# Stick-breaking suffix sums as high and low parts in single-pass matmuls, and the eviction of u moved to VectorE

## The reference

```python
z = jnp.einsum('bqhd,bkhd->bhqk', qb, kb).astype(jnp.float32) * scale
mask = k_pos < q_pos
log_beta = jax.nn.log_sigmoid(z)
log_1m_beta = jnp.where(mask, jax.nn.log_sigmoid(-z), 0.0)
log_remain = lax.cumsum(log_1m_beta, axis=3, reverse=True) - log_1m_beta
att = jnp.where(mask, jnp.exp(log_beta + log_remain), 0.0)
outs.append(jnp.einsum('bhqk,bkhd->bqhd', att.astype(vb.dtype), vb))
...
u = u + (token_shift(u) - u) * mu
```

## Time and profile before

| | |
|---|---|
| median of 3 runs | 1917.1 us (1916.41 to 1917.37) |
| the profiled execution | 1921.47 us, its span 1919.6 us |
| TensorE matmuls, busy | 1825.8 us, 95% of the span |
| TensorE weight loads, busy | 1424.1 us, 74% |
| VectorE, busy | 936.3 us, 49% |
| ScalarE, busy | 697.5 us, 36% |
| GpSimd, busy | 135.3 us, 7% |
| mean TensorE clock granted | 0.98 |

### The profile page before, as it was taken

One profiled execution on the slowest core, in us unless ns is written; L12 is line 12 of the kernel. 1 busy time (PEld: TensorE's weight loads), 2 busy tenths in 40 slices (PEclk: granted clock), 3 DMA queues, 4 the chain that ended last, 5 costly groups with the idle time before them and its releaser, 6 DMA issues.

```text
span 1919.6 us, 27690 instructions
## 1 busy us (share of the span) xinstructions
PE 1825.8 (95%) x11652; PEld 1424.1 (74%) x11652; DVE 936.3 (49%) x1482; ACT 697.5 (36%) x1055; POOL 135.3 (7%) x109
## 2 busy tenths in 40 slices
PE   5998989979999998999999999899889899999999
PEld 2666655758888886788888887565778688888887
DVE  4267877364444344544244444445745544433442
ACT  4224547343323233433133334577311433312321
POOL 0013435200000002000000010000000010000000
PEclk8999999989999999999999999999999899999999
DMA  9663101112222222123223312101000222322231
GB/s 381 235 234 116 45 28 34 66 54 93 95 99 99 99 98 89 66 99 121 73 94 106 113 66 77 66 33 44 24 4 4 66 94 94 123 85 88 98 127 39
DMA packets 44475, 176.16 MB, mean 92 GB/s; under 512 B 5568, under 2 KB 5824, under 8 KB 41024
## 3 DMA queue, kind: packets, MB, share of 16 engines
q1 hardware_dynamic: 44352, 174.39, 26.3%
HBM read 168.34 MB, written 2.10 MB: 89 GB/s over the span
## 4 chain that ended last, share of the span: by engine, by line
PE 85%; DVE 7%; DMA 3%; ACT 3%; issue 2%; SPq 0%; DVEq 0%; ACTq 0%
PE bank L364 23%; PE bank L365 23%; PE bank L366 23%; DMA arena<-ada_late 1%; PE bank L508 1%; PE bank L524 1%; PE bank L540 1%; PE bank L715 1%; PE bank L856 1%; DMA arena<-ada 1%; PE bank L873 1%; PE bank L864 1%; DMA ring<-m_w_v 1%; ACT wsp L1087 1%; DVE arena L2052 1%
## 5 line engine op out<-in xcount | busy, mean ns | idle before, releaser
L1562 DVE TENSOR_TENSOR wsp<-ring,wsp 128x1024 fp32r<-128x1024 f32 (+2 forms) x244 | 312.7, 1283 | 442.4 <-ACT wsp L1087 442.3
L364 PE MATMUL bank<-hs,wsp 128*128 128x512 f32 x1160 | 472.8, 408 | 16.0 <-DVE hs L1829 5.3
L1087 ACT ACTIVATE wsp<-ring 128x1024 fp32r<-128x1024 f32 (+2 forms) x244 | 268.8, 1104 | 579.4 <-PE bank L366 573.4
L365 PE MATMUL bank<-hs,wsp 128*128 128x512 f32 x1160 | 455.0, 392 | 0.0
L366 PE MATMUL bank<-hs,wsp 128*128 128x512 f32 x1160 | 455.0, 392 | 0.0
L364 PEld LDWEIGHTS bank<-hs,wsp 128*128 128x128 f32 x1160 | 219.8, 190 | 87.2 <-issue 31.6
L365 PEld LDWEIGHTS bank<-hs,wsp 128*128 128x128 f32 x1160 | 220.1, 190 | 48.7 <-issue 5.7
L366 PEld LDWEIGHTS bank<-hs,wsp 128*128 128x128 f32 x1160 | 219.6, 189 | 47.1
L365 PE MATMUL bank<-hids,wsp 128*128 128x512 f32 x608 | 236.7, 389 | 0.0
L366 PE MATMUL bank<-hids,wsp 128*128 128x512 f32 x608 | 236.7, 389 | 0.0
L364 PE MATMUL bank<-hids,wsp 128*128 128x512 f32 x608 | 236.7, 389 | 0.0
(11 more groups left out here) (340 smaller groups left out, 2119.2 us busy)
## 6 DMA issues: line engine op xcount, KB each, us to landing
ring<-m_gate SPq DMA_DIRECT2D x44, 512.0 KB, 3.4
ring<-m_up SPq DMA_DIRECT2D x44, 512.0 KB, 3.4
ring<-m_down SPq DMA_DIRECT2D x32, 704.0 KB, 4.0
ring<-m_w_in SPq DMA_DIRECT2D x38, 512.0 KB, 3.5
arena<-ada_late SPq DMA_DIRECT2D x16, 1024.0 KB, 7.1
ring<-m_w_up SPq DMA_DIRECT2D x32, 512.0 KB, 3.4
ring<-m_w_down SPq DMA_DIRECT2D x32, 512.0 KB, 3.4
ring<-m_w_out SPq DMA_DIRECT2D x16, 512.0 KB, 3.7
```

The source lines that it names most:

```text
L364: pe.matmul(out, lhs[0], rhs[0], start=start, stop=False)
L365: pe.matmul(out, lhs[0], rhs[1], start=False, stop=False)
L1087: act.activation(wsp[:, s % SPLIT, 0, 0:size], ring[:, i % RING, 0:size], ACT.Copy)\
L1562: dve.tensor_tensor(wsp[:, s % SPLIT, 1, 0:size], ring[:, i % RING, 0:size], wsp[:, s % SPLIT, 0, 0:size].bitcast(F32), ALU.subtract).then ...
```

## The change

The softplus is kept as two fp32r tensors. VectorE writes it to raw_sp, ScalarE copies it to sp_hi (`sb_high`, new), VectorE subtracts sp_hi from raw_sp into sp_lo, which lies on the same memory as raw_sp. The sums take ramps, an fp32r copy of the two constant matrices, against the high parts of both heads, then against the low parts. The running sums (`presum`) are gone; instead each kind has a matmul per later group of key blocks, widened over unused columns to 256 where there is room. att is one buffer in tmp instead of three. The ScalarE queue gets `sb_high(n)` behind `sb_exp(n-1)`; logs wait for the suffix sum that last read sp_lo. u's first eviction goes from ScalarE to VectorE, as `tensor_scalar` ahead of the shift.

```diff
+        raw_sp = [area(at * K, (2, w)) for at, w in zip((34, 37, 40), WIDTH)]
+        sp_hi = [at(f"sp_hi{n}", [P, 2, w], F32R, arena_at + 4 * k * K)[0] for n, (k, w) in enumerate(zip((24, 27, 30), WIDTH))]
+        sp_lo = [at(f"sp_lo{n}", [P, 2, w], F32R, arena_at + 4 * k * K)[0] for n, (k, w) in enumerate(zip((34, 37, 40), WIDTH))]
+        ramps, _ = at("ramps", [P, 2, P], F32R, cst_at + 4 * CONST["suffix"][0])
+        att = tmp[:, 4:6, :]
...
             def sb_suffix(p):
-                pe.wait_ge(S("softplus"), p + 1)
-                if kind:
-                    pe.wait_ge(S("presum"), 2 * i + kind)
-                for e in range(2):
-                    b = set_of(p) + e
-                    pe.matmul(bank[:, b, 0:w], const("suffix"), sp[kind][:, e, :], start=False, stop=False,
-                              skip_group_check=True)
-                    later = (sp[0][:, e, 0:P], sp[0][:, e, P:3 * P], sp[1][:, e, :])[kind]
-                    at = w - (1, 2, 3)[kind] * P
-                    mm = pe.matmul(bank[:, b, at:w], const("minus"), later, start=False, stop=True,
-                                   skip_group_check=True)
+                later = (((0, 0, 2, 2),), ((0, 1, 1, 2), (0, 0, 2, 2)), ((1, 0, 1, 3), (0, 1, 2, 2), (0, 0, 3, 1)))[kind]
+                for part, v in enumerate((sp_hi, sp_lo)):
+                    if part == 0:
+                        pe.wait_ge(S("sp_hi"), p + 1)
+                    else:
+                        pe.wait_ge(S("softplus"), 2 * p + 2)
+                    for e in range(2):
+                        b = set_of(p) + e
+                        pe.matmul(bank[:, b, 0:w], ramps[:, 0, :], v[kind][:, e, :], start=False, stop=False,
+                                  skip_group_check=True)
+                        for of, at, to, n in later:
+                            mm = pe.matmul(bank[:, b, to * P:(to + n) * P], ramps[:, 1, :],
+                                           v[of][:, e, at * P:(at + n) * P], start=False,
+                                           stop=(part == 1 and of == 0 and at == 0), skip_group_check=True)
                 mm.then_inc(S("sb_suffix"), 1)
...
             def sb_logs(p):
                 if p >= 3:
-                    act.wait_ge(S("sb_pv"), p - 2)
+                    act.wait_ge(S("sb_suffix"), (p, p - 1, p - 2)[kind])
...
+            def sb_high(p):
+                act.wait_ge(S("softplus"), 2 * p + 1)
+                act.activation(sp_hi[p % 3][:, :, :], raw_sp[p % 3], ACT.Copy).then_inc(S("sp_hi"), 1)
...
             def sb_exp(p):
                 act.wait_ge(S("sb_suffix"), p + 1)
-                act.activation(att[kind], bank[:, b:b + 2, 0:WIDTH[kind]], ACT.Exp).then_inc(S("att"), 1)
+                if p:
+                    act.wait_ge(S("sb_pv"), p)
+                act.activation(att[:, :, 0:WIDTH[kind]], bank[:, b:b + 2, 0:WIDTH[kind]], ACT.Exp).then_inc(S("att"), 1)
...
                     sb_exp(n - 1)
+                if n < PARTS:
+                    sb_high(n)
...
-                act.wait_ge(S("u_full"), n + 1)
-                act.activation(u[:, RW_ORDER[n], :], bank[:, n % 2, :], ACT.Identity,
-                               scale=unmixed[:, RW_ORDER[n]:RW_ORDER[n] + 1]).then_inc(S("u_raw"), 1)
...
             def softplus(p):
-                if p >= 3:
-                    dve.wait_ge(S("sb_suffix"), p - 1)
+                own("softplus")
+                dve.wait_ge(S("sp_hi"), p + 1)
+                dve.tensor_tensor(sp_lo[kind][:, :, :], v, sp_hi[kind][:, :, :].bitcast(F32), ALU.subtract)\
+                   .then_inc(S("softplus"), 1)
...
             def token_mix(n):
-                dve.wait_ge(S("u_raw"), n + 1)
+                dve.wait_ge(S("u_full"), n + 1)
+                do(dve.tensor_scalar(f, bank[:, b, :], unmixed[:, RW_ORDER[n]:RW_ORDER[n] + 1], None, ALU.mult))
...
+            do(dve.tensor_copy(ramps[:, :, :].rearrange("p a b -> p (a b)"), cst[:, CONST["suffix"][0]:CONST["minus"][1]]))
             sb_step(0)
```

More of the change, by code:

```diff
@@ L169, in build @@
         arena, arena_at = at("arena", [P, 74 * 256])
-        cst, _ = at("cst", [P, NCONST])
+        cst, cst_at = at("cst", [P, NCONST])
         col, _ = at("col", [P, NCOLS])
@@ L269, in build @@
         WIDTH = (3 * P, 3 * P, T)
-        sp = [area(at * K, (2, w)) for at, w in zip((24, 27, 30), WIDTH)]
-        att = [area(at * K, (2, w)) for at, w in zip((34, 37, 40), WIDTH)]
+        raw_sp = [area(at * K, (2, w)) for at, w in zip((34, 37, 40), WIDTH)]
[3 more added lines that the diff above has]
+        att = tmp[:, 4:6, :]
         u = area(44 * K, (14, T))
@@ L734, in sb_pv @@
                         mm = pe.matmul(bank[DH * e:DH * e + DH, 6, c * P:T], vtok2[:, c, hh * DH:(hh + 1) * DH],
-                                       att[kind][:, e, at:at + w], start=(c == 3), stop=(c == 0), skip_group_check=True)
+                                       att[:, e, at:at + w], start=(c == 3), stop=(c == 0), skip_group_check=True)
                 mm.then_inc(S("sb_pv"), 1)
@@ L1341, in sb_logs @@
                 b, kind = 2 + 2 * (p % 2), p % 3
-                z, raw = att[kind], bank[:, b:b + 2, 0:WIDTH[kind]]
+                z, raw = raw_sp[kind], bank[:, b:b + 2, 0:WIDTH[kind]]
                 act.wait_ge(S("sb_masked"), p + 1)
                 if p >= 3:
-                    act.wait_ge(S("sb_pv"), p - 2)
+                    act.wait_ge(S("sb_suffix"), (p, p - 1, p - 2)[kind])
                 do(act.activation(z, raw, ACT.Abs))
@@ L1444, in _ @@
                     key_line(n - 8)
-                if n >= 10:
-                    act.wait_ge(S("knorm"), n - 9)
-                act.wait_ge(S("u_full"), n + 1)
-                act.activation(u[:, RW_ORDER[n], :], bank[:, n % 2, :], ACT.Identity,
-                               scale=unmixed[:, RW_ORDER[n]:RW_ORDER[n] + 1]).then_inc(S("u_raw"), 1)
                 if 1 <= n < 5:
@@ L1933, in sb_mask @@
                 own("sb_masked")
[L1935 to L1943, removed]
             def softplus(p):
@@ L1947, in softplus @@
                 dve.wait_ge(S("log1p"), p + 1)
-                if p >= 3:
-                    dve.wait_ge(S("sb_suffix"), p - 1)
-                dve.scalar_tensor_tensor(out=sp[kind], in0=bank[:, b:b + 2, 0:WIDTH[kind]], scalar=0.0, in1=att[kind],
+                v = raw_sp[kind]
+                dve.scalar_tensor_tensor(out=v, in0=bank[:, b:b + 2, 0:WIDTH[kind]], scalar=0.0, in1=v,
                                          op0=ALU.max, op1=ALU.add).then_inc(S("softplus"), 1)
+                own("softplus")
+                dve.wait_ge(S("sp_hi"), p + 1)
+                dve.tensor_tensor(sp_lo[kind][:, :, :], v, sp_hi[kind][:, :, :].bitcast(F32), ALU.subtract)\
+                   .then_inc(S("softplus"), 1)
                 own("softplus")
@@ L1962, in sb_step @@
                     sb_mask(n)
-                if 1 <= n <= PARTS and n % 3:
-                    presum(n - 1)
                 if n < PARTS:
```

## The result

The changed kernel takes 1936.15 us in the median of 5 runs (1926.88 to 1937.64), against 1917.1 before. The ratio is 1.0081, with a 95% interval of 1.0061 to 1.0100: slower, as forecast. The forecast was 1931, inside a range of 1921 to 1938. The profiled execution is the fastest of the five, 1926.88 us with a span of 1925.1. This makes the stage, read from a profile, the steadier measure of what happens in it, though not of the kernel's time. From the first part's activations to the start of the last shift of u it took 1368.66 - 1216.79 = 151.9 us before.

The account below looks back on a forecast made before the run. TensorE was taken to bound the stage's first half, VectorE the second, with the ScalarE-VectorE relay becoming the first half's bound. Relay 10.0, second half 2.2 and clock 1.6 gave +13.8 us: median 1931, range 1921 to 1938.

Parts of the forecast that it names:

- What bounds it: Suffix-sum stage: TensorE's time counts in its first half, VectorE's in the second; hardly any slack around 1250 us.
- TensorE's gaps between 1222 and the last sum: Sign of the forecast: TensorE idle 8 us or more in this stretch of the stage.
- The releaser: Sign of the forecast: ScalarE's exponential is what ends TensorE's idle waits before the last sum.
- the waits of 2 and 4 us: First half: TensorE would stop some 2 us for part 1's exponentials and 4 us for part 4's.
- TensorE's part: Suffix sums over four head pairs: TensorE gives back 3.6 us (6.0 with 128 columns at 0.07), if nothing makes it wait.
- The relay, +10.0: First half: alternating ScalarE and VectorE work on each part becomes the bound; last sum begins at 1320.8, before 1310.79.
- The share of the eviction: u's eviction on VectorE: 0.72 us per tile end in the relay; second half +2.2 us, tiles 8 to 11 adding 2.9.
- Clock, +1.6 once: TensorE's clock falls to the 1.2 GHz level after its new wait for part 4, losing 1.6 us once.
- The rival with falls at more stops (1937): Clock falls at parts 1, 4, 6 and 9: two more dips, 3.2 us, high prices 2.5; 1937 us, chance 0.13.
- TensorE's wait for shift 9: Sign of the forecast: TensorE waits 4 us for VectorE's shift 9 of u.
- The rivals of no change and of a gain: TensorE stays the bound: 1917 us, chance 0.12; faster, with cheap 128-column sums and hidden evictions: 1911.5 us, chance 0.05.
- The sum: Whole kernel: 10.0 + 2.2 + 1.6 = +13.8 us, all other work only shifting.

Follow-up runs that it names:

- kernel before with tile ends deferred: Kernel before, with VectorE's work at the end of tiles 0 to 5 moved behind the next part's mask: 1919.6 us, ratio 0.9993.

## Why the prediction came out as it did

- *What bounds it.* Right: TensorE in the first half before, the relay after, VectorE in the second half. One reading of rows is misnumbered: the exponentials that end at 1259.12 and the value matmuls at 1259.26 belong to part 4, not part 3; the slack of 0.1 us that I read from them stands. TensorE's gaps between 1222 and the last sum are 98.5 - 85.3 = 13.2 us by the busy column (at least 8 were expected). The releaser is not the one named: the exponentials released values by 0.3 us, and the waits of 2 and 4 us for those of parts 1 and 4 did not come, because TensorE was already held up at banks 6 and 7.
- *TensorE's part.* The saving was sized too low: 3.6 us were forecast, and the busy times above give 5.9, close to the 6.0 that I kept beside it. The sum of kind 1 took 1.71 us (1.7 forecast), and of kind 2 one pass took 1.33, both 2.7 (2.4 to 3.0 forecast). A group of 384, 256 and 128 columns took 1321.21 - 1320.86 = 0.35 us, which leaves 0.06 for 128 columns: I took 0.22 and should have taken 0.07. By the Trainium skill's four passes for full FP32 ("FP8 and Floating Point Precision", TensorE Precision Notes) it was a quarter of 0.22; the trace agrees. The time forecast would still not have been better by it: it would have lain 2 us lower, farther from what was measured.
- *The relay, +10.0.* The mechanism held, but **this term was mis-sized: the first half grew by 15.0**, where relay and clock together were to give 11.6. Its prices are right (high 0.84, low 0.96, eviction 0.74), and the first two groups miss by 0.3 and 0.7 us. The third misses by 3.1 and the fourth by 1.2. What failed is that I let only logs of kind 0 lead over TensorE. The orders on record have the new high part ahead of `osb_squares` and `osb_root`; I priced these as ScalarE's time alone, though they also free banks 6 and 7 for TensorE's values and kk product. The reordering of ScalarE alone recovers 3.1 us. From part 6 to 7 it took 12.55 us for 10.65, of which 1.74 are the mask's wait for scores.
- *The share of the eviction.* In the second half +2.2 was forecast, with 0.57 for the eviction of tile 7, whose row reads 0.67; measured are +2.7 after and 3.1 to 3.2 when the eviction is moved alone. In the first half the relay's sum held 0.72 us for each tile end, but taking it out returned 1.3 us in all.
- *Clock, +1.6 once.* This was too small. In the first half the clock stood at 0.50 from the first sum at 1216.15 up to 1222, and again behind both stops of 3.2 us; TensorE needed some 6.8 us more for the same work than at 0.98. How much of that is on the path no run tells, since none takes the clock apart from the stops. The rival with falls at more stops (1937) is nearest to the median, 1936.15. TensorE's wait for shift 9 was forecast at 4 us and is 4.13:

```profile
1356.95 0.80 PE L367 MATMUL bank<-hs,wsp 128*128 128x512 f32 x1 [4.13 <-DVE arena L1974]
```

- *The rivals of no change and of a gain.* Their mechanisms exist. They need the relay out of the way, which the change does not do; the version with high part, eviction and raw softplus moved does, and has a stage 1.5 us shorter than before.
- *The sum.* Its +13.8 is close to the 14.0 us by which the changed kernel's median lies above that of the kernel before when both run by turns. That is luck in part: the stage grew by 17.7, which the time does not show in full, and the forecast had put no change outside the stage.

In stage time the loss is 17.7 us: 9.6 for high and low part with their hand-overs, 3.5 for the eviction moved alone, and 4.6 for what is left between 155.4 and 160.0. The split depends on the order in which the pieces are taken: the eviction returns 4.5 us from the changed kernel and 5.8 once the high part is on VectorE. The memory shared by raw and low part accounts for 3.1 of the 4.6 if its worth in the changed kernel holds here; the other 1.5 I can't place (one att tile for all kinds is a candidate that was not tried). The median moved by 14.0 to 19.0 us against the kernel before on the respective chip.

## What to carry to other kernels

Cheaper work on the busiest engine pays only if what prepares it on the others stays shorter than that engine's time: lay out one round of the hand-overs, operation by operation, before trusting busy shares of 43% and 73%. In that round follow every bank and every buffer, not only the data: an operation put ahead of the one that frees a bank ties another engine in, and prices then no longer add. When the split is wanted, do softplus, high and low on one engine, which gave 8.4 us of stage here, and put the rest of that engine's queue into its waits.

## What the runs showed of the hardware

- VectorE's copy to fp32r is twice as fast per element as its subtraction: 0.29 us for 256 elements, 0.56 for 768 and 0.69 for 1024, so 0.52 ns an element, against 0.96 and 1.23 for 768 and 1024, 1.05 ns. It beats ScalarE's 0.84 for 768 as well. The Trainium skill ("VectorE: DVE Perf Modes", What auto-detection actually checks) gives a doubled rate to one source and a destination in SBUF and not to fp32 with two sources; the trace agrees.
- A single-pass matmul takes 0.06 us for 128 columns, where the f32 one takes 0.22, and 0.23 for 512, where it takes 0.85. Within a pass of the last sum, the two matmuls of 512 columns took 0.34 and 0.28 to the next start (1320.52 to 1320.86, 1321.21 to 1321.49).
- In the changed kernel the granted clock was 0.50, the 1.2 GHz level, behind idle times of 3.27, 3.17 and 4.13 us of TensorE, and 1.00 behind 2.70 and 1.49 us (at 1301.5 and 1312.2). The length of the idle time is not all that counts: in the version with the high part on VectorE and the eviction on ScalarE it was 0.53 behind 2.25 us.
- Executions of the same code start the stage at different times, 1211.5 to 1225.7 us over fourteen profiles. The start follows the clock granted to TensorE from 130 to 300 us (0.98, 0.97 and 0.90 in the changed kernel, the kernel before and the kernel before with tile ends deferred, whose code up to there does the same work and whose stages start at 1211.5, 1216.8 and 1225.7 us):

```profile
130.00:300.00 170.00, 157.35 (x1162) 108.19 (x1160) 135.05 (x413) 89.00 (x234) 70.09 (x64) 0.98 0.17 56
```

```profile
130.00:300.00 170.00, 157.07 (x1116) 108.02 (x1112) 134.17 (x405) 83.42 (x218) 66.04 (x61) 0.97 0.19 63
```

```profile
130.00:300.00 170.00, 158.29 (x1050) 110.19 (x1050) 127.78 (x382) 77.09 (x198) 63.18 (x58) 0.90 0.19 63
```

Why the chip grants less there in one execution than in another no run here tells. It is why I compare distances within the stage, which repeat to 0.1 us in the two profiles of the changed kernel.
